# A ring of expert weights begun one stage earlier, the last pair of experts kept on the chip, and filler products on TensorE

## The reference, cut to what matters

```python
# first block
cap = EC_CAPACITY_FACTOR * T // N_EXPERTS                    # 64
aff = jax.nn.softmax((h @ w_router).astype(jnp.float32), axis=-1)
gate, idx = lax.top_k(jnp.transpose(aff, (0, 2, 1)), cap)
hid = silu(xg @ w_eg) * (xg @ w_eu);  yo = (hid @ w_ed) * gate;  out = zeros.at[idx].add(yo)
# second block
x = x + merged @ w_out[l]                                    # "output projection"
h2 = rmsnorm(x, ffn_norm_g[l])
g_sel = argmax(softmax(h2 @ w_group + b_group)); top_v, top_i = lax.top_k(fine_sel, 2)
gate = softmax(top_v) * gate_g
x = x + sum over the 2 experts of gate * ((silu(gt) * up) @ w_down[e]),  gt, up = split(h2 @ w_gu[e])
return rmsnorm(x, final_norm_g)
```

## Time and profile before

| | us |
|---|---|
| runs shown, median (lowest to highest) | 3594.27 (3591.18 to 3597.16) |
| profiled execution, its own time | 3598.31 |
| its span | 3596.5 |
| TensorE busy (15792 products) | 3148.0, 88% |
| weight loads of TensorE | 1667.6, 46% |
| VectorE, ScalarE, GpSimd busy | 1070.2, 558.9, 286.4 |

### The profile page before, as it was taken

The page is one execution under the profiler, slowest core; times in us unless marked ns, Lnnn a source line. Parts: engine busy times, 40 slices in busy tenths (PEclk is TensorE's granted clock), DMA queues, the critical chain, the costliest instruction groups (busy, mean ns, idle before and its releaser), DMA issues. The chain is left out here.

```text
span 3596.5 us, 37828 instructions
## 1 busy us (share of the span) xinstructions
PE 3148.0 (88%) x15792; PEld 1667.6 (46%) x15792; DVE 1070.2 (30%) x2063; ACT 558.9 (16%) x1178; POOL 286.4 (8%) x270
## 2 busy tenths in 40 slices
PE   6997889998899999698999999987996789995984
PEld 5444645664554444453344434433545763643331
DVE  2233702454573301410111011103056553522112
ACT  2002510112452200100000000002022221301111
POOL 0003000002761000000000000000002200001000
PEclk9998998998899999699999999998998999996997
DMA  7721021110001222379999999996310021017996
GB/s 264 257 71 47 2 74 35 47 36 0 24 1 47 94 70 70 164 295 428 424 425 428 424 424 412 421 423 277 128 35 2 3 109 49 12 59 275 404 425 259
DMA packets 132079, 669.33 MB, mean 186 GB/s; under 512 B 17578, under 2 KB 45645, under 8 KB 98889
## 3 DMA queue, kind: packets, MB, share of 16 engines
q1 hardware_dynamic: 115385, 630.24, 43.5%
q10 hardware_dynamic: 11488, 28.31, 2.1%
q0 software_dynamic: 5040, 8.40, 0.7%
HBM read 672.15 MB, written 14.69 MB: 191 GB/s over the span
## 5 line engine op out<-in xcount | busy, mean ns | idle before, releaser
L1992 PE MATMUL ec_wide<-ec_ring,ec_xg 128*64 128x512 f32 x2048 | 456.7, 600 | 20.8 <-issue 15.4
L1992 PEld LDWEIGHTS ec_wide<-ec_ring,ec_xg 128*64 128x64 f32 x2048 | 148.1, 138 | 309.3 <-issue 305.1
L2026 PE MATMUL ec_acc<-ec_ring,ec_hidT 128*64 128x512 f32 x1024 | 238.8, 622 | 36.4 <-DMA ec_ring<-in_w_exp_down 34.5
L2151 DVE TENSOR_SCALAR ec_xg<-ec_piece,ordered 128x128 f32<-128x128 f32 x64 | 21.9, 405 | 579.7 <-PE ec_piece L2040 579.7
L2026 PEld LDWEIGHTS ec_acc<-ec_ring,ec_hidT 128*64 128x64 f32 x1024 | 84.9, 143 | 188.1 <-issue 188.1
L3677 PE MATMUL hm_gu<-hm_ring,hm_xg 128*64 128x512 f32 x512 | 121.3, 629 | 15.8 <-DMA hm_ring<-in_moe_w_gu,hm_again_rows 7.7
L2040 PEld LDWEIGHTS ec_piece<-ec_sel,x 128*128 128x128 f32 x512 | 122.9, 336 | 8.6 <-issue 5.7
L2040 PE MATMUL ec_piece<-ec_sel,x 128*128 128x128 f32 x512 | 124.4, 406 | 2.8 <-DVE ec_sel L2133 2.8
L2727 POOL TENSOR_TENSOR solve_T<-const_rw,solve_T 128x512 f32<-128x512 f32 x8 | 10.1, 1266 | 1321.3 <-DVE solve_T L2765 1321.3
L2115 ACT ACTIVATE ec_hidT<-ec_acc 128x512 f32<-128x512 f32 x32 | 17.4, 594 | 516.1 <-PE ec_acc L2015 516.1
L1141 PE MATMUL conv_main<-hT,conv_early 128*128 128x512 f32 x192 | 86.2, 605 | 1.6 <-DVE bcT L1217 1.6
(11 more groups left out here) (624 smaller groups left out, 4957.3 us busy)
## 6 DMA issues: line engine op xcount, KB each, us to landing
ec_ring<-in_w_exp_gate SPq DMA_DIRECT2D x64, 2048.0 KB, 13.6
ec_ring<-in_w_exp_up SPq DMA_DIRECT2D x64, 2048.0 KB, 22.2
ec_ring<-in_w_exp_down SPq DMA_DIRECT2D x64, 2048.0 KB, 17.3
hm_ring<-in_moe_w_gu SPq DMA_DIRECT2D x32, 2048.0 KB, 27.3
hm_ring<-in_moe_w_down SPq DMA_DIRECT2D x16, 2048.0 KB, 29.1
ahead_qkv<-in_w_in SPq DMA_DIRECT2D x10, 2048.0 KB, 9.6
key<-in_w_ada ACTq DMA_DIRECT2D x4, 2048.0 KB, 8.7
v<-in_w_ada ACTq DMA_DIRECT2D x4, 2048.0 KB, 10.2
```

Source lines behind the costliest of these rows:

```text
L1992: last = pe.matmul(wide[half(e), b, :], xg[:, u % 2, j, half(e)], w[e][:, a, b * 512:(b + 1) * 512], start=(j == 0), stop=(j == KD - 1))
L2026: last = pe.matmul(acc[half(e), h, :], hidT[:, f, half(e)], w[e][:, r, h * 512:(h + 1) * 512], start=(f == 0), stop=(f == FT - 1))
```

## The change

1. The first ring has 8 places instead of 7.
2. The second ring's first seven places (HM_HEAD = 7) are allotted before the output projection and their pieces are asked for in it. The eighth place is a new tile `hm_ring_late`, the ninth is `u2T`, which the projection has finished reading; these two are asked for in the router's stage, ahead of the rows' store. `second_mixer` is moved out one level of indentation for that (not shown).
3. The last pair of experts is not stored. Its one-hot marks, multiplied by the gates, are turned and kept in `hm_sel`; TensorE spreads the pair's rows `hm_y` over the tokens by products with them, and VectorE adds these from PSUM. The eight fetches wait for 15 pairs instead of 16; row numbers of the last pair are out of range for them and their factor is zero (`earlier`).
4. `keep_clocked` issues products of the constants `ones` and `ident` into a PSUM bank that nothing reads: 12 and 72 in the first router, 12 in the second experts.
5. The final norm loads ScalarE's table of roots first and takes each tile's root by itself.

```diff
+def keep_clocked(k, pe, bank, n):
+    for _ in range(n):
+        pe.matmul(bank[:, 0:P], k.const("ones"), k.const("ident"), start=True, stop=True)
...
-EC_SLOTS = 7
+EC_SLOTS = 8
...
+HM_HEAD = HM_SLOTS - 2
...
+        self.head = scope.enter_context(k.nc.sbuf_tensor("hm_ring", [P, HM_HEAD, PIECE], F32))
+        self.places = [self.head[:, n, :] for n in range(HM_HEAD)] + [None, last]
...
             norm.turn(pe, scores)
+            keep_clocked(k, pe, norm.pt[:, 0, :], 12)
             pe.wait_ge(aff_ready, 1)
             for t in range(LT):
                 last = pe.transpose(wide[0:E, t * P:(t + 1) * P], aff[:, t, :], k.const("ident"))
             last.then_inc(wide_ready, 1)
+            keep_clocked(k, pe, norm.pt[:, 0, :], 72)
             pe.wait_ge(chosen_T, 1)
...
+    k.rounds_ring = RoundsRing(k, k.second_scope, uT[:, :, :].rearrange("p j n -> p (j n)"))
+    project_rows_onto(k, "p_out2", k.dram["w_out_2"][0], KD, uT, k.residual, 2, ahead,
+                      also=lambda sp: k.rounds_ring.load_first(sp, range(HM_HEAD)))
...
-            ring.load_first(sp, range(3))
+            ring.load_first(sp, range(HM_HEAD, HM_SLOTS))
             sp.wait_ge(norm.row_ready, LT)
             sp.dma_start(xn_rows.rearrange("(t p) d -> p t d", p=P), norm.xn[:, :, :]).then_inc(xn_stored, 16)
-            ring.load_first(sp, range(3, HM_SLOTS))
...
-            for b in range(2):
-                pool.wait_ge(y_stored[b], 16 * HM_PAIRS // 2)
-            pool.wait_ge(down_done, HM_PAIRS)
+            pool.wait_ge(y_stored[0], 16 * (HM_PAIRS // 2))
+            pool.wait_ge(y_stored[1], 16 * (HM_PAIRS // 2 - 1))
+            pool.wait_ge(down_done, HM_PAIRS - 1)
...
             lists(1)
+            pe.wait_ge(index_ready, 2)
+            keep_clocked(k, pe, list_, 12)
             flips(0)
...
+                if u == HM_PAIRS - 1:
+                    pe.wait_ge(weighted, 2)
+                    for t in range(LT):
+                        last = pe.transpose(list_[:, t * P:(t + 1) * P], sel[:, u % 2, t, :], k.const("ident"))
+                    last.then_inc(weights_turned, 1)
                 if u:
                     down(u - 1)
+            pe.wait_ge(weights_ready, 1)
+            pe.wait_ge(y_ready, HM_PAIRS)
+            for t in range(LT):
+                if t >= 2:
+                    pe.wait_ge(added, 3 * (t - 2) + 3)
+                for h in range(2):
+                    last = pe.matmul(combined[t % 2][:, h, :], sel[:, HM_PAIRS % 2, t, :], y[:, (HM_PAIRS - 1) % 2, h * 512:(h + 1) * 512],
+                                     start=True, stop=True)
+                last.then_inc(last_product, 1)
...
+                if u == HM_PAIRS - 1:
+                    act.wait_ge(weights_turned, 1)
+                    act.activation(sel[:, HM_PAIRS % 2, :, :].rearrange("p t n -> p (t n)"), list_[:, :], ACT.Copy).then_inc(weights_ready, 1)
...
+            for t in range(LT):
+                for i in range(2):
+                    dve.wait_ge(fetched[2 * t + i], 16)
...
+                    dve.scalar_tensor_tensor(out[:, t, :], back[:, 2 * t + i, :], earlier[:, i, t:t + 1], out[:, t, :], ALU.mult, ALU.add).then_inc(added, 1)
+                dve.wait_ge(last_product, t + 1)
+                dve.wait_ge(added, 3 * t + 2)
+                dve.tensor_tensor(out[:, t, :], out[:, t, :], combined[t % 2][:, :, :].rearrange("p b n -> p (b n)"), ALU.add).then_inc(added, 1)
...
+            act.preload_act_table(ACT.Sqrt)
             for t in range(LT):
                 link(act.activation(square[:, :], x[:, t, :], ACT.Square, accum_out=ss[:, t:t + 1]))
-            act.activation(rstd[:, :], ss[:, :], ACT.Sqrt, scale=1.0 / D, bias=k.const("eps")).then_inc(root_ready, 1)
+                act.activation(rstd[:, t:t + 1], ss[:, t:t + 1], ACT.Sqrt, scale=1.0 / D, bias=k.const("eps")).then_inc(root_ready, 1)
```

More of the change, by code:

```diff
@@ L1623, in wait_loaded @@
         dve.wait_ge(residual.loaded, 16)
-    project(k, label, w, kt, 512, n_chunks, groups, add, ahead=ahead, first=wait_loaded)
+    project(k, label, w, kt, 512, n_chunks, groups, add, ahead=ahead, first=wait_loaded, also=also)
 def project_rows(k, label, w, kt, xT, out, n_chunks, width=512, ahead=None, then=None, also=None):
@@ L1871, with __init__ @@
 class RoundsRing:
-    def __init__(self, k, scope):
+    def __init__(self, k, scope, last):
         self.k = k
@@ L1912, in load @@
     def load(self, sp, n):
-        sp.dma_start(*second_weights(self.k, self.tile[:, n % HM_SLOTS, :], *self.order[n])).then_inc(self.loaded[n % HM_SLOTS], 16)
+        sp.dma_start(*second_weights(self.k, self.places[n % HM_SLOTS], *self.order[n])).then_inc(self.loaded[n % HM_SLOTS], 16)
     def wait(self, pe, *job):
@@ L1921, in wait @@
             pe.wait_ge(self.loaded[n % HM_SLOTS], 16 * (n // HM_SLOTS))
-        return self.tile[:, n % HM_SLOTS, :]
+        return self.places[n % HM_SLOTS]
 def stream_experts(k, ring, x, rstd, rank, gate, scale_cols, shift_cols, out):
@@ L3606, in fine_experts @@
         BACK = 2 * LT
-        back = ring.tile[:, 0:BACK * D // PIECE, :].rearrange("p s (b n) -> p (s b) n", n=D)
+        last_rows = HM_E * SLOTS - 2 * SLOTS
+        weight, earlier = sb("weight", [P, 2, 2, LT]), sb("earlier", [P, 2, LT])
+        back = ring.head[:, 3:3 + BACK * D // PIECE, :].rearrange("p s (b n) -> p (s b) n", n=D)
         gu, turn, acc, flip, list_ = ps("gu", [P, 2, 512]), ps("turn", [P, 512]), ps("acc", [P, 2, 512]), ps("flip", [P, 2, 512]), ps("list", [P, 512])
+        combined = [gu, acc]
         blank, half_ready, sel_ready, listed, index_ready, flipped, xg_ready = (
@@ L3642, in _ @@
             pool.wait_ge(source_ready, 1)
[L3643 to L3645 removed]
+            pool.wait_ge(y_stored[0], 16 * (HM_PAIRS // 2))
+            pool.wait_ge(y_stored[1], 16 * (HM_PAIRS // 2 - 1))
+            pool.wait_ge(down_done, HM_PAIRS - 1)
             for n in range(BACK):
[L3647 to L3648 removed]
+                pool.indirect_dma_start(back[:, n, :], None, y_rows, bass.IndirectOffsetOnAxis(ap=source[:, n % 2, n // 2:n // 2 + 1], axis=0),
+                                        bounds_check=last_rows - 1, oob_is_err=False).then_inc(fetched[n], 16)
         @block.tensor
@@ L3757, in gathered_tokens, with last_weights @@
                                   scale_cols.unsqueeze(2).to_broadcast([P, KD, P]), ALU.mult).then_inc(xg_ready, 1)
+            def last_weights():
+                u = HM_PAIRS - 1
+                for e in range(2):
+                    link(dve.scalar_tensor_tensor(weight[:, e], first[:, :, :], float((2 * u + e) * SLOTS - 1), here[:, :, :], ALU.is_equal, ALU.mult))
+                    link(dve.tensor_tensor(weight[:, e, 0, :], weight[:, e, 0, :], weight[:, e, 1, :], ALU.add))
+                    dve.tensor_tensor(sel[:, u % 2, :, half(e)], sel[:, u % 2, :, half(e)],
+                                      weight[:, e, 0, :].unsqueeze(2).to_broadcast([P, LT, SLOTS]), ALU.mult).then_inc(weighted, 1)
+                link(dve.scalar_tensor_tensor(earlier[:, :, :], first[:, :, :], float(last_rows) - 1.5, here[:, :, :], ALU.is_lt, ALU.mult))
             one_hots(0)
@@ L3836, in second_experts @@
         out = k.residual.tile
-        with ExitStack() as s:
-            ring = RoundsRing(k, s)
+        with k.second_scope as s:
+            ring = k.rounds_ring
+            ring.complete(s)
             ordered = tile(s, "hm_ordered", [P, KD])
```

220 lines of the change are left out of this document (109 added, 111 removed).

## The result

| | before | after |
|---|---|---|
| median of four runs each (first comparison) | 3593.66 us | 3564.34 us |
| ratio, 95% interval | | 0.9919 [0.9901, 0.9936] |
| a later comparison (e12 below) | 3596.95 us | 3565.95 us, ratio 0.9917 [0.9901, 0.9933] |
| profiled execution: span, mean granted clock | 3596.5 us, 0.931 | 3561.0 us, 0.944 |

The two profiled executions differ by 35.5 us, more than the medians, since that of before was a long one (3598.31 against 3593.66) and that of after a short one (3562.81 against 3564.34).

A forecast was written before the change was run, and what follows sets the result against it. Bounds: full DMA engines in the first experts, idle DMA in the router, a late second start, and a tail of fetches, sums and norm. Terms -4.9 + 3.8 - 9.9 - 1.0 - 1.3 - 2.3 = -15.6 gave 3579 us, range 3569 to 3591.

The forecast's parts named there:

- the first ring: First experts' weight ring: an eighth place loads one more piece in idle time; -4.9 us, bounds -2.2 and -4.9.
- First router: Fillers in the first router delay the marks, partly given back by counts at twice the clock; net +3.8 us.
- (b): First router: fillers are harmless, fitting in the wait for VectorE; -2.5 instead of +3.8, total 3572 us; chance 0.16.
- (c): First router: the clock does not rise, or filler records take 0.243 us; 3601 us at most; chance 0.12.
- (d): First router: each filler's load and product run one after the other, at least 0.336 us a record; 3616 us; chance 0.07.
- Second start: Second experts' begin: with nothing queued, gather and empty copies land sooner, first product starts earlier; -9.9 us.
- rival (a): Second experts' begin: GpSimd's descriptors, not full queues, make copies and gathers slow, gaining 0; 3590 us; chance 0.13.
- First product's clock: Second experts' first product spends less at the lower clock after a shorter gap; -1.0 us.
- Last pair: Tail: last pair kept in SBUF, fetches start one store earlier, VectorE then sets the end; -1.3 us.
- Norm: Final norm: table loaded first, each tile's root taken by itself; -2.3 us, bounds 0 and -3.0.

The follow-up runs named there:

- e12: The changed kernel measured once more, nothing altered, on the chip of the last group; 3566.0 us, ratio 0.9917 to the kernel before.
- e1: The kernel before with eight places instead of seven in the first experts' ring, nothing else changed; 3578.6 us, ratio 0.9957 to the kernel before.
- e2: The changed kernel with seven places instead of eight in the first experts' ring; 3583.7 us, +19.4 on the changed kernel.
- e3: The changed kernel without the 12 and 72 filler products of the first router; 3562.7 us, -1.7 on the changed kernel.
- e6: The changed kernel with the second ring's weights asked for in the router, as before, none in the output projection; 3574.1 us, +9.8.
- e7: The changed kernel without the 12 filler products ahead of the second experts' first turns; 3570.7 us, ratio 0.9935 to the kernel before.
- e8: The changed kernel with the last pair's rows stored and fetched like the others' and the old final norm; 3571.7 us, ratio 0.9938 to the kernel before.
- e10: The changed kernel plus 28 and 18 fillers in the second router and GpSimd's clearing of the gathered rows' place in two halves; 3567.9 us.
- e11: The changed kernel with 0 and 50 first-router fillers, e10's changes, final gain loaded during the last pair, table load behind ScalarE's last expert copy; 3560.9 us.

## Why the prediction was wrong

**The step that failed is the first ring:** "Same pieces and bytes, one more loaded in time that is idle. The later loads start with the first free place as before, but one fewer is left: -4.9", with bounds of -2.2 and -4.9. It took the DMA engines as full and so left one piece as the only thing that an eighth place could give. What it measured is -16.0 alone (e1; -11.8 in the stretch of its trace), +19.4 when taken back (e2), -13.3 in the stretch of the two first traces. What took the term's place is a shortage of outstanding loads at each gather: besides the one piece, 1.2 to 2.5 us in each pair. The fault is in how was read: the mean of one pair of seven, with 425 GB/s and a share of 1.00. The page's own slices had 412 and 421 in the same stage, and later pairs took 120.96 and 119.76 us. The share hardly shows a dip, 0.98 or 0.99 at 400 to 414 GB/s; the rate does. The bounds were drawn from that same row, so they didn't hold the answer either. Of the 13.7 us by which the gain was larger than forecast, 8.4 are this term by the traces and 11.1 by e1's median.

**First router, +3.8:** +3.15 and +2.85 in the traces of the changed kernel and of e12. Right in mechanism and near in size, with 0.213 and 0.113 us a record. By e3 nothing comes back behind the counts. Rivals (b), (c) and (d) of the fillers fall: they cost, the clock rose, and a record cost 0.113, far from 0.25.

**Second start, -9.9:** -10.3 in the trace, 10.1 undone by e6. The path came as written: no backlog, gather in 4.5 us, turns behind the fillers. (The bounds do not come out of their rows: a copy of 9 us gives -6.0 and not -5.6, and free fillers would leave the copy's landing at 3298.2, -10.3 and not -10.9.) The copies landed in 2 to 3 us, below the 4.7 used, which changed nothing since the scaling was last. The rule cited beside rival (a), from the Trainium skill (DMA: Bandwidth & Descriptors, "Queues, rings and completion order"), is that an engine takes packets in turn from the queues that have work. Rival (a) read it so that a copy without data would pass another queue's backlog; e6 and the changed kernel differ in that backlog alone, and the copies take 12.8 against 2.1 to 2.7 us. Here they do wait for it.

**First product's clock, -1.0:** mis-sized, -2.4 (9.49 to 7.09 us), and 2.8 by e7 (9.85). I halved an effect that the fillers removed whole. The 1.7 us that the following products gained beside it were in no term.

**Last pair, -1.3:** -1.1 by e8, -1.1 to -1.8 from the last but one pair's store on, e10 left out. The step "from there VectorE, not the fetches, sets the end" is what the trace shows. Nearly all of the other 1.35 of the -2.5 in the table is the last pair's first product, whose 9.97 us held more of the lower clock (the hidden rows' turn starts 9.90 us behind its start before and 8.60 after); no term had it.

**Norm, -2.3:** -2.4, and 1.7 to 2.4 with the other profiles of the same norm. The parts as written add to 3589.2, not 3589.4; the rest of the term was an allowance for the gain's load, and the first row did wait for that load. By the Trainium skill (ScalarE: Activation LUTs, "What ACT_TABLE_LOAD costs", 2.66 us in all) it would have been -0.9; the next operation starts 1.30 us after the load's start in both kernels, so the trace does not agree, and the measurement decides.

With e1's median for the ring and the traces' sizes for the rest, -16.0 + 3.0 - 10.3 - 2.4 - 1.7 - 1.1 - 2.4 = -30.9, against -29.3 and -31.0 in the two comparisons; with the traces' -11.8 or -13.3 for the ring it is -26.7 or -28.2. The terms cover the gain within what can be told. With -13.3 in place of -4.9 and all else as forecast the sum is -24.0, which is 3570, just inside the range: the ring is most of the miss, and the clock of the products, named above, most of the rest.

## To carry to other kernels

Full DMA engines in one window don't show that a ring is deep enough: look at every period, in windows about as long as the stretch in which the consumer releases nothing (20 us here, for 15.55), at the rate and not only at the share, and at how long loads take from issue to landing, which with the rate counts the loads outstanding. A place more was here worth one piece once and the dips in every period; going from seven to six cost more per pair (3.9 us) than going from eight to seven (2.5). Fillers should fill a wait and end with it: too many put their excess on the path, and they are sized from the two prices of a record and the length of the wait.

## What the runs showed of the hardware

- The clock can fall in a short wait, and not always does. Behind the same 56 records and the same wait of 2.7 us the 20 count records took 2.42 us in e10 and 4.48 in e11:

```profile
3262.42 2.42 PE L3524 MATMUL hm_choose_count<-hm_choose_chosen,const_all 128*128 128x32 f32 x20 [2.70 <-DVE hm_choose_chosen L3584]
```

```profile
3252.24 4.48 PE L3523 MATMUL hm_choose_count<-hm_choose_chosen,const_all 128*128 128x32 f32 x20 [2.69 <-DVE hm_choose_chosen L3583]
```

- In the first experts a group of 32 records that starts behind a wait of 2.7 us for its weights takes 7.09 us in some places and 8.78 in others, here both in the kernel before. The row of the group doesn't show what makes the difference.

```profile
1681.43 8.78 PE L2026 MATMUL ec_acc<-ec_ring,ec_hidT 128*64 128x512 f32 x32 [2.70 <-DMA ec_ring<-in_w_exp_down]
...
1918.54 7.09 PE L2026 MATMUL ec_acc<-ec_ring,ec_hidT 128*64 128x512 f32 x32 [2.70 <-DMA ec_ring<-in_w_exp_down]
```

- A store of 512 KB landed 4.5 us after its issue where a load of 512 KB (one row spread to 128 partitions) had been issued 1.1 us ahead of it in another queue (e11), and 2.6 us after it without that load (the changed kernel, e10; DMA issues view). It is one store in one run; no experiment takes the load out alone.
